# A two-layer decoder step: the first loads in another order, and the working area moved by one small tensor

## The chip, the cores and the metric

One core of a Trainium2 chip runs the whole step as one program. The metric is the device time in microseconds of one execution, the median of several; the profile comes from one further execution.

## What is computed

Two layers of a hybrid decoder, for one prompt of 256 tokens and 8 decode requests of one token each, so 264 rows of width 1024, all in float32. Cut to what matters here:

```python
q, k, v, z, xbc, dt = jnp.split(x @ w_in, IN_SPLITS, axis=-1)
q = _rope(q.reshape(b, L, 2 * ATT_HEADS, ATT_QK_DIM), pos)
k = _rope(k.reshape(b, L, 2 * ATT_HEADS, ATT_QK_DIM), pos)
...
dt = jax.nn.softplus(dt.astype(jnp.float32) + dt_bias.astype(jnp.float32))
...
mk, mv = jnp.split(mem @ w_ckv, 2, axis=-1)
...
logits = (x @ w_router).astype(jnp.float32)      # layer 1 only
top_v, top_i = lax.top_k(logits, TOP_K)
```

A layer is the mixer (differential attention beside a state space model, both from one input projection), cross-attention over 256 memory rows, and a feed-forward stage: dense in layer 0, the two best of eight experts in layer 1. Each of the three ends in a layer norm.

## The kernel before

Five engines run five hand-written instruction lists that meet at semaphores. TensorE (PE) multiplies, VectorE (DVE), ScalarE (ACT) and GpSimd (POOL) work on the results, and SyncE (SP) issues the loads. All weights pass through `ring`, six slots of 16 KB in each partition; `ring_chunks` lists the chunks in order and, for each, after which group of products its slot is free again. Results of TensorE go through eight PSUM banks; `psum_groups` lists the groups in order, with the engine (`"V"` or `"A"`) that empties each, and group n waits until group n - 8 has been emptied. So the order of both lists is the order of the work.

The start is this. SP issues `const` (identity, masks, cosines: 564 KB), the layer norm and convolution vectors into `vraw` (six small DMAs), x (slot 0), the memory rows (slot 1), the page table `ptab`, the q columns of `w_in` (slot 2), then nine small loads that all count on `small_landed` (the per-head parameters `raw8` and `col8`, the lambda parameters `lraw`, the time step weights `wdt` of both layers and the router's weights `wr`), then the columns k, xbc0, xbc1, the pages of cached keys, v and z. TensorE waits for `const` and the vectors, transposes the vectors (`vec`), x (`xin`, five groups by `blocks8`) and the memory rows (`mem`, four groups). Then the mixer begins: `token_major` multiplies the columns q and k by the decode rows and by two tiles of 128 prompt rows (`DECODE_FIRST` is that order: 2, 0, 1). After the decode rows of q come the time step products `dt`, 48 of 8 columns and 16 more, which wait for `small_landed`. After k come the cumulative sums (`acs`), and then eight blocks of xbc with the scores over the cached keys between them.

DVE copies `xin` to `xT` and spreads the decode rows over `xs` (`decode_columns`, line 2333). ACT copies `mem` to `memT`. Both then wait for `small_landed` for the parameters' set-up. GpSimd sets buffers to zero, waits for `const`, loads the convolution state (line 889), rotates q and k once they are there (lines 902 to 907), and stores k.

Most of the later time is products of layer 1's experts: their weights are cut into a high and a low part by ACT (line 1772) and DVE (line 2155), and TensorE (line 1216 is the line of all products, line 1220 of all transposes) multiplies three pairs of parts. The tiles of that stage lie in `arena`, the working area, which the stages of the kernel use in turn. `x_high`, `x_low` and `first_high` of layer 0's feed-forward stage lie in `arena` also; `high` lies in `R`, `SQ` and `memT`. The tensors stand one behind another in the order of their declarations.

Of the kernel before, what the change touches and what calls it, by code (L numbers as in the profile page):

```python
# [27 lines left out]
I32 = mybir.dt.int32  # L28
ALU = mybir.AluOpType
# [358 lines left out]
def build(nc, a, outs, lots=SLOTS, always=False):  # L388
# [3 lines left out]
    with ExitStack() as ctx:  # L392
# [67 lines left out]
        vraw = carve(2 * P, 0).rearrange("p (a n) -> p a n", a=2)  # L460
        lraw = carve(L * 4 * DQ).rearrange("p (l a d) -> p l a d", l=L, a=4)
# [144 lines left out]
        psum_full, emptied_by_act, emptied_by_dve = sem("psum_full"), sem("emptied_by_act"), sem("emptied_by_dve")  # L606
        const_landed, vecs_landed, small_landed, ptab_landed = (
# [77 lines left out]
        def _(sp):  # L685
            sp.dma_start(const[:], a["consts"]).then_inc(const_landed, 16)
            for j, (src, r0) in enumerate((
                    (a["ln_g"].rearrange("l i (k n) -> (l i k) n", n=P), 0),
                    (a["ln_b"].rearrange("l i (k n) -> (l i k) n", n=P), 48),
                    (a["ssm_norm_w"].rearrange("l (k n) -> (l k) n", n=P), 96),  # L690
                    (a["attn_norm_w"], 104),
                    (a["conv_b"].rearrange("l (k n) -> (l k) n", n=P), 106))):
                sp.dma_start(vraw[r0:r0 + src.shape[0], 0, :], src).then_inc(vecs_landed, 16)
            sp.dma_start(vraw[0:64, 1, :], a["conv_w"].rearrange("l i (k n) -> (l i k) n", n=P)
                         ).then_inc(vecs_landed, 16)
# [26 lines left out]
            for l in range(L):  # L722
                w_in = a["w_in"][l]
                columns((l, "q"), w_in, 0)
                if l == 0:
                    for i, n in enumerate(("dt_bias", "a_log", "d_skip")):
                        sp.dma_start(raw8[:, i], a[n].partition_broadcast(P)).then_inc(small_landed, 16)  # L727
                    with nc.allow_non_contiguous_dma(reason="sixteen words"):
                        for i, n in enumerate(("dt_bias", "a_log")):
                            sp.dma_start(col8[:, i, :], a[n].rearrange("l h -> h l")).then_inc(small_landed, 16)  # L730
                    sp.dma_start(lraw, a["lambda_params"].partition_broadcast(P)).then_inc(small_landed, 16)
# [4 lines left out]
                for key, c0 in (("k", 512), ("xbc0", 2048), ("xbc1", 2560)):  # L736
                    columns((l, key), w_in, c0)
# [2052 lines left out]
```

## Time and profile before

| | us |
|---|---|
| median of three runs | 1812.07 (1811.1 to 1814.3) |
| the profiled execution | 1809.09 |
| its span, from first to last instruction | 1807.2 |

The profiled execution was faster than the three timed ones. Its granted TensorE clock was 0.993 on average. TensorE was busy for 97% of the span, DVE 68%, ACT 47%, GpSimd 6%. The chain of work that ended last is followed back from the last instruction to what released each step; a timeline lists an engine's work in order, and ends a line with what the engine had waited for; a table by stretches gives each engine's busy time, the granted clock as a share of 2.4 GHz, and what the DMA engines did.

### The profile page before, as it was taken

How to read it: one execution, taken by the hardware profiler on the slowest of the kernel's cores; microseconds unless marked ns; L12 is line 12 of the kernel's file. 1: busy time of each engine (PE TensorE's matmuls, PEld its weight loads, DVE VectorE, ACT ScalarE, POOL GpSimd, SP SyncE). 2: the span in 40 equal slices, each digit the busy share in tenths (PEclk: the TensorE clock that was granted, in tenths of full speed). 3: DMA queues.
4: the chain of work that ended last, by engine and by line, in shares of the span. 5: the costliest groups of instructions: out<-in, count | busy, mean ns of one | idle time of the engine just before them, and what ended most of it. 6: DMA issues, size and time to landing. Idle time of an engine off the chain costs nothing.

```text
span 1807.2 us, 24014 instructions
## 1 busy us (share of the span) xinstructions
PE 1760.1 (97%) x8760; PEld 1360.8 (75%) x8760; DVE 1225.6 (68%) x1739; ACT 852.8 (47%) x978; POOL 112.2 (6%) x120
## 2 busy tenths in 40 slices
PE   7999999999999999999999999999999999999998
PEld 4646587789999565568677878878888878878786
DVE  2687636255544288543626989898988989898984
ACT  1122211154442122302205777777777777777774
POOL 0530000000000332000001000000000000000000
PEclk9999999999999999999998999999999999999999
DMA  9556544845526455563682989999999999999980
GB/s 323 183 199 212 215 185 169 285 158 181 175 83 228 137 185 171 187 262 123 233 279 96 358 279 356 345 348 352 349 376 324 377 324 363 337 350 352 348 335 26
DMA packets 300436, 459.34 MB, mean 254 GB/s; under 512 B 10879, under 2 KB 213817, under 8 KB 300343
## 3 DMA queue, kind: packets, MB, share of 16 engines
q1 hardware_dynamic: 294630, 442.63, 71.6%
q0 software_dynamic: 3424, 11.50, 1.9%
q10 hardware_dynamic: 2304, 4.20, 0.6%
q8 instruction: 47, 0.77, 0.2%
q14 instruction: 31, 0.25, 0.0%
HBM read 444.97 MB, written 13.46 MB: 254 GB/s over the span
## 4 chain that ended last, share of the span: by engine, by line
PE 86%; DVE 7%; ACT 3%; issue 1%; DMA 1%; SPq 1%; POOL 0%; ACTq 0%; DVEq 0%; POOLq 0%
PE bank L1216 83%; PE bank L1220 3%; DVE arena L2682 1%; DVE ring_low L2155 1%; ACT high L1772 1%; DMA out<-mem_rows 1%; DVE R L2296 1%; ACT L1772 0%; ACT arena L1840 0%; POOL arena L964 0%; ACT ye_high L1808 0%; ACT SQ L1861 0%; DVE st L2654 0%; DVE st L2575 0%; SPq L727 0%
## 5 line engine op out<-in xcount | busy, mean ns | idle before, releaser
L2155 DVE TENSOR_TENSOR ring_low<-ring,high 128x2048 fp32r<-128x2048 f32 x264 | 603.0, 2292 | 87.0 <-ACT high L1772 84.0
L1772 ACT ACTIVATE high<-ring 128x2048 fp32r<-128x2048 f32 x264 | 505.3, 1917 | 110.7 <-PE bank L1216 101.5
L1216 PE MATMUL bank<-high,xg_high 128*128 128x512 f32 x704 | 285.0, 405 | 6.2 <-DVE ring_low L2155 5.8
L1216 PE MATMUL bank<-ring_low,xg_high 128*128 128x512 f32 x704 | 278.5, 396 | 0.0
L1216 PE MATMUL bank<-high,xg_low 128*128 128x512 f32 x704 | 278.2, 395 | 0.0
L1216 PEld LDWEIGHTS bank<-high,xg_high 128*128 128x128 f32 x704 | 132.4, 188 | 36.3 <-DVE ring_low L2155 7.3
L1216 PEld LDWEIGHTS bank<-ring_low,xg_high 128*128 128x128 f32 x704 | 132.2, 188 | 31.7
L1216 PEld LDWEIGHTS bank<-high,xg_low 128*128 128x128 f32 x704 | 132.5, 188 | 28.4
L1840 ACT ACTIVATE arena<-bank 128x512 f32<-128x512 f32 (+3 forms) x95 | 46.4, 525 | 218.4 <-PE bank L1216 142.8
L1216 PE MATMUL bank<-high,he_high 128*128 128x512 f32 x352 | 141.8, 403 | 0.0
L1216 PE MATMUL bank<-ring_low,he_high 128*128 128x512 f32 x352 | 139.2, 396 | 0.0
L1216 PE MATMUL bank<-high,he_low 128*128 128x512 f32 x352 | 139.1, 395 | 0.0
L2273 DVE TENSOR_TENSOR ring_low<-ring,high 128x2048 fp32r<-128x2048 f32 (+1 forms) x32 | 71.1, 2225 | 92.6 <-ACT high L1849 92.6
L1216 PE MATMUL bank<-xT,ring 128*128 128x264 f32 x512 | 120.3, 391 | 0.8 <-ACT xT L1876 0.8
L1216 PE MATMUL bank<-SQ,ring 128*128 128x264 f32 x512 | 116.6, 391 | 0.9 <-issue 0.7
L1216 PE MATMUL bank<-ring,xT 128*128 128x512 f32 x256 | 116.5, 613 | 0.0
L1216 PE MATMUL bank<-ring,memT 128*128 128x512 f32 x256 | 113.3, 595 | 0.0
L1216 PEld LDWEIGHTS bank<-SQ,ring 128*128 128x128 f32 x512 | 98.1, 192 | 18.7 <-DVE SQ L2643 0.9
L1216 PEld LDWEIGHTS bank<-xT,ring 128*128 128x128 f32 x512 | 95.2, 190 | 21.9 <-issue 4.4
L1216 PE MATMUL bank<-x_high,ring_low 128*128 128x264 f32 x352 | 99.9, 284 | 0.0
L1849 ACT ACTIVATE high<-ring 128x2048 fp32r<-128x2048 f32 (+1 forms) x32 | 59.6, 1864 | 82.9 <-PE bank L1216 82.0
L1216 PEld LDWEIGHTS bank<-ring,xT 128*128 128x128 f32 x256 | 49.3, 196 | 62.6 <-issue 62.5
(327 smaller groups left out, 2613.2 us busy)
## 6 DMA issues: line engine op xcount, KB each, us to landing
ring<-in_w_exp_gu SPq DMA_DIRECT2D x176, 1024.0 KB, 11.3
ring<-in_w_exp_down SPq DMA_DIRECT2D x40, 2048.0 KB, 14.2
ring<-in_w_in SPq DMA_DIRECT2D x12, 2048.0 KB, 9.7
ring<-in_w_ffn_gu SPq DMA_DIRECT2D x22, 1024.0 KB, 8.5
ring<-in_w_ckv SPq DMA_DIRECT2D x8, 2048.0 KB, 8.6
ring<-in_cache_mem_k SPq DMA_DIRECT2D x16, 1024.0 KB, 8.1
ring<-in_cache_mem_v SPq DMA_DIRECT2D x16, 1024.0 KB, 6.6
ring<-in_cache_attn_k SPq DMA_DIRECT2D x32, 256.0 KB, 3.5
```

The source lines that it names most:

```text
L1216: return M.matmul(out, lhsT, rhs, start=start, stop=stop)
L1220: return M.transpose(out, in_, ident[0:n, 0:n])
L1772: S.activation(high_bufs[h % HIGH_BUFS][:], ring[:, s, j * HALF:(j + 1) * HALF], ACT.Copy).then_inc(split_high, 1)
L1840: emptied_after(name, S.activation(dst, src(bk), func))
L1849: S.activation(high, ring[:, s, part], ACT.Copy).then_inc(ffn_high, 1)
L2155: V.tensor_tensor(ring_low[:, s, part], ring[:, s, part], high_bufs[h % HIGH_BUFS][:], ALU.subtract).then_inc(split_low, 1)
L2273: V.tensor_tensor(ring_low[:, s, part], ring[:, s, part], high, ALU.subtract).then_inc(ffn_low, 1)
L2296: V.scalar_tensor_tensor(R[:, k, :], R[:, k, :], col_g(l, i, k), stat[:], ALU.mult, ALU.mult).then_inc(scaled.sem, 1)
L2682: ins = V.scalar_tensor_tensor(ctmp[:, (2 * t + j) * MD:(2 * t + j + 1) * MD], Kb[:, t, h * MD:(h + 1) * MD], 1.0, bk[:, j * MD:(j + 1) * ...
```

## The change

SP loads the identity alone, then x, then q. The rest of `const` and the vectors follow q, then k, and the memory rows and the page table follow k. The memory rows are the fourth chunk of the ring instead of the second. GpSimd issues seven of the nine small loads, at its start (layer 0's time step weights first); the other two, layer 1's time step weights and the router's, it issues after layer 0's rotated keys, and they count on `thin_landed`, for which layer 1 waits. TensorE transposes x first, and the vectors and the memory rows between k and the cumulative sums; their copies by DVE and ACT move along, and so do the copy of `pick` and the scaling of the attention norm. `dt` stands behind the first prompt tile of q, in both layers. ACT copies two of the five groups of x. `vraw` lies at the end of the working area, and `slot_token`, four bytes in each partition, is declared behind `arena` instead of ahead of it. The diff, cut:

```diff
 def psum_groups():
-    g = [(("vec",), "V")]
-    g += [(("xin", n), "V") for n in range(5)] + [(("mem", n), "A") for n in range(4)]
+    g = [(("xin", n), "A" if n in (1, 3) else "V") for n in range(5)]
...
-                if c == "q" and t == DECODE_FIRST[0]:
+                if c == "q" and t == DECODE_FIRST[1]:
                     add("V", "dt")
+                if l == 0 and c == "k" and t == DECODE_FIRST[-1]:
+                    g += [(("vec",), "V")] + [(("mem", n), "A") for n in range(4)]
...
 def ring_chunks():
-    c = [(("x",), 2, "pe", ("xin", 4)), (("mem",), 1, "pe", ("mem", 3))]
+    c = [(("x",), 2, "pe", ("xin", 4))]
     for l in range(L):
-        c += [((l, n), 1, "pe", (l, "tok", n, DECODE_FIRST[-1])) for n in ("q", "k")]
+        c += [((l, "q"), 1, "pe", (l, "tok", "q", DECODE_FIRST[-1]))]
+        c += [((l, "k"), 1, "pe", (l, "tok", "k", DECODE_FIRST[-1]))]
+        if l == 0:
+            c += [(("mem",), 1, "pe", ("mem", 3))]
...
-        slot_token = sb("slot_token", [P, 1], I32)
         x_rows = nc.dram_tensor("x_rows", [T, D], F32).ap()
         arena = sb("arena", [P, ARENA])
+        slot_token = sb("slot_token", [P, 1], I32)
...
-        vraw = carve(2 * P, 0).rearrange("p (a n) -> p a n", a=2)
-        lraw = carve(L * 4 * DQ).rearrange("p (l a d) -> p l a d", l=L, a=4)
+        vraw = carve(2 * P, ARENA - 2 * P).rearrange("p (a n) -> p a n", a=2)
+        lraw = carve(L * 4 * DQ, 0).rearrange("p (l a d) -> p l a d", l=L, a=4)
...
         @block.sync
         def _(sp):
-            sp.dma_start(const[:], a["consts"]).then_inc(const_landed, 16)
-            for j, (src, r0) in enumerate((
...
+            sp.dma_start(const[:, C_ID:C_ID + P], a["consts"][:, C_ID:C_ID + P]).then_inc(ident_landed, 16)
             s = rg.claim(sp, ("x",))
...
-            s = rg.claim(sp, ("mem",))
-            sp.dma_start(ring[:, s, 0:2048].rearrange("p (t n) -> p t n", t=2),
-                         a["mem_prompt"].rearrange("o (t p) n -> p (o t) n", p=P)).then_inc(landed[s], 16)
-            sp.dma_start(ptab[:], a["page_table"].rearrange("b g -> (b g)").unsqueeze(0)).then_inc(ptab_landed, 16)
+            def first_vectors():
+                sp.dma_start(const[:, C_ID + P:NCONST], a["consts"][:, C_ID + P:NCONST]).then_inc(const_landed, 16)
...
+            def memory_rows():
+                s = rg.claim(sp, ("mem",))
...
                 columns((l, "q"), w_in, 0)
                 if l == 0:
-                    for i, n in enumerate(("dt_bias", "a_log", "d_skip")):
-                        sp.dma_start(raw8[:, i], a[n].partition_broadcast(P)).then_inc(small_landed, 16)
...
-                    for n in range(L):
-                        sp.dma_start(wdt[:, n], a["w_in"][n, :, 3072:3080].rearrange("(k p) n -> p k n", p=P)
-                                     ).then_inc(small_landed, 16)
-                    sp.dma_start(wr[:], a["w_router"][0].rearrange("(k p) n -> p k n", p=P)).then_inc(small_landed, 16)
-                for key, c0 in (("k", 512), ("xbc0", 2048), ("xbc1", 2560)):
+                    first_vectors()
+                columns((l, "k"), w_in, 512)
+                if l == 0:
+                    memory_rows()
+                for key, c0 in (("xbc0", 2048), ("xbc1", 2560)):
                     columns((l, key), w_in, c0)
...
             G.memset(xpad[:, :, 0:3], 0.0).then_inc(buffers_set, 1)
+            def time_step_weights(n, landed_by):
+                pool.dma_start(wdt[:, n], a["w_in"][n, :, 3072:3080].rearrange("(k p) n -> p k n", p=P)
+                               ).then_inc(landed_by, 16)
+            time_step_weights(0, small_landed)
+            for i, n in enumerate(("dt_bias", "a_log", "d_skip")):
+                pool.dma_start(raw8[:, i], a[n].partition_broadcast(P)).then_inc(small_landed, 16)
...
+            pool.dma_start(lraw, a["lambda_params"].partition_broadcast(P)).then_inc(small_landed, 16)
             pool.wait_ge(const_landed, 16)
...
                 store(o_ks[l, :, 0].rearrange("b h d -> b (h d)"), qkr[0:8, 2, 512:1024])
+                if l == 0:
+                    time_step_weights(1, thin_landed)
+                    pool.dma_start(wr[:], a["w_router"][0].rearrange("(k p) n -> p k n", p=P)).then_inc(thin_landed, 16)
...
-            pe.wait_ge(const_landed, 16)
-            pe.wait_ge(vecs_landed, 16 * 6)
...
+            pe.wait_ge(ident_landed, 16)
             blocks8(("xin",), slot(("x",))[:, 0:3072].rearrange("p (t n) -> p t n", t=3))
...
                         token_major(c, t, first)
-                        if first:
-                            pe.wait_ge(small_landed, 16 * 9)
+                        if c == "q" and t == DECODE_FIRST[1]:
+                            pe.wait_ge(*((thin_landed, 16 * 2) if l else (small_landed, 16 * 7)))
                             bk = turns.open(pe, (l, "dt"))
...
+                    if l == 0 and c == "k":
+                        vector_columns()
+                        memory_columns()
                 bk = turns.open(pe, (l, "acs"))
+                pe.wait_ge(const_landed, 16)
...
-            for n in range(4):
-                copy_out(("mem", n), memT[:, 4 * (n % 2):4 * (n % 2) + 4, (n // 2) * P:(n // 2 + 1) * P],
+            for n in (1, 3):
+                copy_out(("xin", n), xT[:, 4:8, (n // 2) * P:(n // 2 + 1) * P],
                          lambda bk: bk[:].rearrange("p (k n) -> p k n", k=4))
-            act.wait_ge(small_landed, 16 * 9)
+            act.wait_ge(small_landed, 16 * 7)
...
+                if l == 0:
+                    bk = take(dve, ("vec",))
+                    step.inc(V.tensor_copy(vecT[:, 0, 0:122], bk[:, 0:122]))
+                    emptied_after(("vec",), V.tensor_copy(vecT[:, 1, 0:64], bk[:, 128:192]))
...
```

## Rows read from the trace of the kernel before

**Rows 1.** The page, part 4: shares of the chain that ended last, by engine.

```profile
PE 86%; DVE 7%; ACT 3%; issue 1%; DMA 1%; SPq 1%; POOL 0%; ACTq 0%; DVEq 0%; POOLq 0%
```

**Rows 2.** The chain that ended last, in order of time: start us, us, what.

```profile
17.43 4.01 DMA wr<-in_w_router
21.48 38.04 PE bank L1216 x152
...
64.16 44.71 PE bank L1216 x184
...
252.99 1.75 PE bank L1220 x16
```

**Rows 3.** Timeline of SP's queue: start us, us, line, operation, out<-in, count.

```profile
0.76 0.42 SPq L686 DMA_DIRECT2D const<-in_consts  x1
...
3.83 0.58 SPq L697 DMA_DIRECT2D ring<-in_x_prompt  x1
...
6.09 2.90 SPq L727 DMA_DIRECT2D raw<-in_dt_bias  x1
...
25.84 21.71 SPq L718 DMA_DIRECT2D ring<-in_cache_attn_k  x16
```

**Rows 4.** Timeline of PE, first 60 us, and one row of layer 1.

```profile
9.67 8.23 PE L1220 MATMUL bank<-const,ring 128*128 128x128 f32 x40 [3.17 <-DMA ring<-in_x_sample]
18.79 1.92 PE L1216 MATMUL bank<-ring,mem_rows 128*32 128x512 f32 x16 [0.89 <-issue]
21.48 4.43 PE L1216 MATMUL bank<-wdt,xT 128*128 128x8 f32 x48 [0.77 <-DMA wr<-in_w_router]
...
26.25 16.68 PE L1216 MATMUL bank<-ring,xT 128*128 128x512 f32 x32
42.86 1.92 PE L1216 MATMUL bank<-ring,mem_rows 128*32 128x512 f32 x16
44.72 14.00 PE L1216 MATMUL bank<-ring,xT 128*128 128x512 f32 x32
...
595.70 4.54 PE L1216 MATMUL bank<-ring,xT 128*128 128x512 f32 x7
```

**Rows 5.** Timeline of DVE: the decode rows' columns.

```profile
14.59 0.20 DVE L2333 COPY mem_rows<-xT 128x64 f32<-128x64 f32 x1
```

**Rows 6.** Stretches of the start: busy us of each engine, granted clock, DMA share, GB/s.

```profile
6.00:9.00 3.00, 0.50 (x2) 0.18 (x1) 0.58 (x3) 0.00 (x0) 0.29 (x1) 1.00 1.03 397
9.00:12.00 3.00, 2.33 (x11) 2.33 (x12) 1.01 (x2) 0.00 (x0) 0.00 (x0) 1.00 0.99 295
12.50:17.00 4.50, 4.50 (x25) 4.15 (x25) 1.81 (x4) 1.20 (x2) 0.00 (x0) 1.00 1.05 386
17.00:18.00 1.00, 0.90 (x5) 0.50 (x3) 0.00 (x0) 0.66 (x2) 0.00 (x0) 1.00 1.11 354
18.00:21.00 3.00, 1.92 (x16) 0.50 (x16) 0.00 (x0) 0.54 (x1) 0.00 (x0) 1.00 0.88 104
```

**Rows 7.** Stretches again, for the clock, in the same columns.

```profile
9.70:13.10 3.40, 3.40 (x16) 3.25 (x16) 1.95 (x3) 0.00 (x0) 0.00 (x0) 1.00 1.02 322
...
24.90:31.60 6.70, 6.70 (x42) 3.54 (x43) 3.41 (x10) 0.80 (x3) 0.00 (x0) 0.50 1.05 393
...
594.90:598.20 3.30, 3.30 (x35) 1.94 (x35) 1.00 (x6) 0.46 (x2) 0.00 (x0) 0.50 0.33 90
```

**Rows 8.** POOL's timeline, and of the same line its DMAs' time from issue to landing.

```profile
5.02 0.72 POOL L889 DMA_DIRECT2D SQ<-in_state_conv  x1 [2.94 <-DMA const<-in_consts]
...
DMA to landing us min/median/max: 6.0/6.6/7.2
```

**Rows 9.** Tile x_high: duration of its products in ns, min/median/max.

```profile
L1216 PE MATMUL bank<-x_high,high x320: 279/283/290, 392.4 to 508.6; 128*128 128x264 f32 x160
...
L1216 PE MATMUL bank<-x_high,first_high x32: 281/284/361, 380.6 to 392.1; 128*128 128x264 f32 x32
```

**Rows 10.** The page, part 5: one of the groups of the experts' products.

```profile
L1216 PE MATMUL bank<-high,xg_high 128*128 128x512 f32 x704 | 285.0, 405 | 6.2 <-DVE ring_low L2155 5.8
```

More of the change, by code:

```diff
@@ L883, in _ @@
             G.memset(xpad[:, :, 0:3], 0.0).then_inc(buffers_set, 1)
+            def time_step_weights(n, landed_by):
[4 more added lines that the diff above has]
+                pool.dma_start(raw8[:, i], a[n].partition_broadcast(P)).then_inc(small_landed, 16)
+            with nc.allow_non_contiguous_dma(reason="sixteen words"):
+                for i, n in enumerate(("dt_bias", "a_log")):
+                    pool.dma_start(col8[:, i, :], a[n].rearrange("l h -> h l")).then_inc(small_landed, 16)
+            pool.dma_start(lraw, a["lambda_params"].partition_broadcast(P)).then_inc(small_landed, 16)
             pool.wait_ge(const_landed, 16)
@@ L1321, in x_ready, with vector_columns, memory_columns @@
                 return ready
-            pe.wait_ge(const_landed, 16)
-            pe.wait_ge(vecs_landed, 16 * 6)
-            bk = turns.open(pe, ("vec",))
-            tr(bk[:, 0:122], vraw[0:122, 0, :], 122)
-            full(tr(bk[:, 128:192], vraw[0:64, 1, :], 64))
-            blocks8(("xin",), slot(("x",))[:, 0:3072].rearrange("p (t n) -> p t n", t=3))
-            mem_in = slot(("mem",))[:, 0:2048].rearrange("p (t n) -> p t n", t=2)
-            for n in range(4):
-                bk = turns.open(pe, ("mem", n))
-                for j in range(4):
-                    k = 4 * (n % 2) + j
-                    last = tr(bk[:, j * P:(j + 1) * P], mem_in[:, n // 2, k * P:(k + 1) * P], P)
-                full(last)
+            pe.wait_ge(ident_landed, 16)
+            blocks8(("xin",), slot(("x",))[:, 0:3072].rearrange("p (t n) -> p t n", t=3))
+            def vector_columns():
+                pe.wait_ge(vecs_landed, 16 * 6)
+                bk = turns.open(pe, ("vec",))
+                tr(bk[:, 0:122], vraw[0:122, 0, :], 122)
+                full(tr(bk[:, 128:192], vraw[0:64, 1, :], 64))
+            def memory_columns():
+                mem_in = slot(("mem",))[:, 0:2048].rearrange("p (t n) -> p t n", t=2)
+                for n in range(4):
+                    bk = turns.open(pe, ("mem", n))
+                    for j in range(4):
+                        k = 4 * (n % 2) + j
+                        last = tr(bk[:, j * P:(j + 1) * P], mem_in[:, n // 2, k * P:(k + 1) * P], P)
+                    full(last)
+            copied(pe, ("xin", 3))
             pe.wait_ge(buffers_set, 6)
@@ L1880, in _ @@
             S.preload_act_table_set(EXP_AND_LN)
-            for n in range(4):
-                copy_out(("mem", n), memT[:, 4 * (n % 2):4 * (n % 2) + 4, (n // 2) * P:(n // 2 + 1) * P],
+            for n in (1, 3):
+                copy_out(("xin", n), xT[:, 4:8, (n // 2) * P:(n // 2 + 1) * P],
                          lambda bk: bk[:].rearrange("p (k n) -> p k n", k=4))
-            act.wait_ge(small_landed, 16 * 9)
+            act.wait_ge(small_landed, 16 * 7)
             step.inc(S.activation(raw8[:, 1], raw8[:, 1], ACT.Exp))
@@ L1913, in _ @@
                             copy_out((l, "tok", name, t), qk_raw[:, t, 512 * c:512 * (c + 1)], lambda bk: bk[:])
+                    if l == 0 and c == 1:
+                        for n in range(4):
+                            copy_out(("mem", n), memT[:, 4 * (n % 2):4 * (n % 2) + 4, (n // 2) * P:(n // 2 + 1) * P],
+                                     lambda bk: bk[:].rearrange("p (k n) -> p k n", k=4))
                 decays_in.wait(act, l)
@@ L2318, in _ @@
             step.inc(V.memset(xs, 0.0))
-            bk = take(dve, ("vec",))
-            step.done(V.tensor_copy(pick[:], const[0:40, C_PICK:C_PICK + 8]))
-            step.inc(V.tensor_copy(vecT[:, 0, 0:122], bk[:, 0:122]))
-            emptied_after(("vec",), V.tensor_copy(vecT[:, 1, 0:64], bk[:, 128:192]))
-            for n in range(5):
+            for n in (0, 2, 4):
                 t, bk = n // 2, take(dve, ("xin", n))
@@ L2326, in _ @@
                 nk = 8 if t == 2 else 4
-                k0 = 0 if t == 2 else 4 * (n % 2)
                 emptied_after(("xin", n), V.tensor_copy(
-                    xT[:, k0:k0 + nk, t0:t0 + rows], bk[:, 0:nk * rows].rearrange("p (k n) -> p k n", k=nk)))
+                    xT[:, 0:nk, t0:t0 + rows], bk[:, 0:nk * rows].rearrange("p (k n) -> p k n", k=nk)))
             def decode_columns(l):
@@ L2391, in _ @@
                 other_quarters(1, "k", qk_raw[0:8, 2, 512:1024])
+                if l == 0:
+                    bk = take(dve, ("vec",))
+                    step.inc(V.tensor_copy(vecT[:, 0, 0:122], bk[:, 0:122]))
+                    emptied_after(("vec",), V.tensor_copy(vecT[:, 1, 0:64], bk[:, 128:192]))
+                    dve.wait_ge(const_landed, 16)
+                    step.done(V.tensor_copy(pick[:], const[0:40, C_PICK:C_PICK + 8]))
+                    for n in range(L):
+                        step.inc(V.tensor_scalar(col_attn(n), col_attn(n), 1.0 - LAM_INIT[n], None, ALU.mult))
                 bk = take(dve, (l, "acs"))
```

31 lines of the change are left out of this document (16 added, 15 removed).

## The prediction

> **What bounds the kernel now.** I read the chain of work that ended last first: 86% of the span is TensorE [Rows 1]. Nearly all of it is products behind one another, so a change of loads can only pay where TensorE waits for a load. Followed from its start, the chain is SP's queue and then the router's weight load `wr`, issued at 17.43 and in use at 21.48; from there it is TensorE without a break for 38.04 us, and again for 44.71 us from 64.16 [Rows 2]. So the only stretch that this change can shorten ends at 21.48, and what it adds to TensorE's own work between 21.48 and 58.7 costs its full length. After that SP issues a load when TensorE frees a slot, so the rest of the kernel should move as one block with the end of k.
>
> Second, the timelines. SP issues `const` at 0.76, seven DMAs on x at 3.83, and the first load after q at 6.09 [Rows 3]. TensorE transposes x and the memory rows from 9.67 to 17.9, begins q at 18.79, stops 0.77 us at the time step weights (`dt`), and goes on at 21.48 [Rows 4]. The decode columns that q needs were ready at 14.79 [Rows 5], so the wait up to 18.79 is for q's bytes. The stretches by DMA rate say the same: 295 to 397 GB/s until 18, then 104 GB/s [Rows 6]. The DMA engines are full until q is in, and x's consumer waits for x. The start is bound by bytes in front of q and by SP's order, not by TensorE.
>
> Third, the clock. The 16 transposes between 9.7 and 13.1 took 3.40 us, 0.21 us each [Rows 7], against 0.109 us at 252.99 (16 in 1.75 us) [Rows 2]. They ran at 1.2 GHz, although the column says 1.00 there (I take it that no change had been recorded yet). The first q products took 1.92 us, as those at 42.86 did [Rows 4], so 2.4 GHz had been reached by then. After the narrow `dt` products the granted clock is 0.50 from 24.9 to 31.6 [Rows 7]: two prompt tiles of q take 16.68 us where k's two take 14.00 [Rows 4], 2.68 us lost. In layer 1 the same happens from 594.9 to 598.2 [Rows 7], while full products run from 595.70 [Rows 4], which is about 1.3 us lost.
>
> **x earlier.** Only the identity (64 KB, one issue like const's 0.42 us) stays before x, so x is issued at about 0.76 + 0.42 + 0.05 = 1.23 instead of 3.83 [Rows 3]. All behind it moves by 2.6 us: x is used at 7.07 instead of 9.67, and the decode columns are ready at 12.2 instead of 14.8 [Rows 4, 5]. ScalarE's two copies of x take the place of DVE's and cost nothing: ScalarE has only its table load before.
>
> **q earlier.** The 1 MB of memory rows and `const` leave the way before q. The last q byte to the first product took 18.79 - 18.0 = 0.8 us [Rows 4, 6]; x's last byte then lies near 7.07 - 0.8 = 6.3. q is 2.1 MB, at 386 to 397 GB/s [Rows 6] 5.4 us, so it is usable at 6.3 + 5.4 + 0.8 = 12.5 if nothing else runs. But GpSimd now issues seven loads from 2.1 us on (it idles from there, 2.94 us before 5.02 [Rows 8]), and they share the engines with x and q: 0.3 MB, of which 1024 pieces of 32 bytes. At q's rate that is 0.7 us. From above: with the three loads of such small pieces in it, 18 to 21 moved at 104 GB/s, so one of the three cost about 1 us; and from 9 to 12, while GpSimd's own two DMAs ran, the rate was 295 instead of 390, which over q's 5.4 us is 1.8 us; with lambda's 0.7, 3.5 in all. I take 1.6, nearer to the low end since the measured dip lasted 3 us. q starts at **14.1** (12.5 to 16.0) instead of 18.79: **4.7 us won** (2.8 to 6.3).
>
> **dt without the wait.** The router's weights and layer 1's time step weights are no longer waited for: 0.77 us won [Rows 4]. `dt` now stands behind a prompt tile of q, so it is wanted at about 14.1 + 1.9 + 7.0 + 2 = 25. GpSimd's issue of a small load took 0.72 us and its landing 6.0 to 7.2 us [Rows 8]: seven issues end near 2.1 + 7 x 0.72 = 7.1, and land near 14.3. Cover is 10 us. ScalarE and DVE wait for them too, with only q's decode quarter behind that wait; its bank is not wanted back before eight more groups. The work of `dt`, 21.48 to 26.25, stays as long in its new place, in both layers.
>
> **Transposes onto the path.** The 16 of the memory rows and the two of the vectors lay under the wait for q; now they stand between k and the cumulative sums, with nothing to hide them: 16 x 0.109 = 1.75 [Rows 2] and about 0.3 for the two others, **2.05 lost**. Their copies (four of ScalarE, two and three small ones of DVE) run beside them and beside the sums, and are free unless ScalarE's last copy delays its one exponential there, some tenths.
>
> **The clock.** Transposes of x alone last 4.4 us instead of 8.2, and 2 us without work follow, so I expect q to begin at 1.2 GHz. Price: the stretches after `dt`, 2.7 and 1.3 us, mean **2.0 lost** (0 to 2.7). After `dt` the clock should fall as before; its mean price is 2.0, 0.7 less than what this profile paid: **0.7 won** (0 to 1.4).
>
> The Trainium skill (TensorE: Matmul & The Clock Gate, Part 4) says that transposes don't count as busy for the clock. Here they did: nothing but transposes ran from 9.67 to 17.9, and the products behind them were at full speed [Rows 4]. By the page, q would have begun slow in the kernel before also, and this term would be 0.
>
> **Slots.** x, q, k and memory rows now lie in slots 0 to 3. The second half of the cached keys waits for q's slot, free near 38; eight of the 16 pages take half of 21.71 us [Rows 3], so they are issued by 49, before k ends. v waits for k's slot, and is read only after the stretch that began at 64.16 [Rows 2]. GpSimd's two later loads stand behind the rotation, before its wait for the state; SP no longer issues them. All nothing.
>
> **The working area.** Each tensor starts at a multiple of 32 bytes; by the sizes, `arena` starts 32 bytes past a multiple of 64 and would start on one. In the feed-forward stage weights that lie in `arena` (`first_high`) and weights on multiples of 64 (`high`) meet the same moving rows: 284 and 283 ns [Rows 9]. The moving rows of 1056 bytes lie by turns on and off such a multiple, and all of them take 279 to 293 ns. So 0 to 1 ns; over the experts' three groups of 704 and three of 352 products [Rows 10] at most 3.2 us won. No row shows a loss from either start. I take 0.
>
> **Sum.** 4.7 + 0.77 - 2.05 - 2.0 + 0.7 = **2.1 us won**. The profiled run took 1809.09 us (span 1807.2), so it would take 1807.0; the median of the runs shown is 3 us above it, and 1812.07 - 2.1 gives **1810.0**. Best ends together: 6.3 + 0.77 - 2.05 + 1.4 = 6.4 won, 1805.7. Worst ends: 2.8 + 0.77 - 2.05 - 2.7 = -1.2, 1813.3.
>
> **Rivals.** (a) *The start pays in full*: GpSimd's loads fall behind q, or the clock rises in x's transposes. 5 to 6.4 us, **about 1806.5**. For it: q at 12.5 needs only the bytes; against it the dip at 9 to 12 [Rows 6].
> (b) *GpSimd's queue takes the place of `wr`* (slower): seven loads through its queue, waited for together. Should each take its 6.6 us after the one before, the last lands at 2.1 + 46 = 48, 23 us after `dt` wants it: **1833**. It decides from 25 us on, and from 31 on the kernel is slower by more than can be told. Against it: 10 us of cover. The Trainium skill (DMA: Bandwidth & Descriptors, Issuing engine by pattern) speaks for it: simple loads belong on SP, whose path is generally faster than GpSimd's. In this trace GpSimd's load needs 7.2 us with x and q in flight, which agrees.
> (c) *q isn't earlier at all*, since it is the DMA engines that count and GpSimd's small pieces cost what the memory rows did: only the transposes move, 2.05 - 0.77 = 1.3 lost, **1813.4**.
> (d) *The working area's start matters* where no row here shows it: experts' products with their weights there. 3 us or more, **1807 or below**.
>
> **Chances.** Forecast 0.53, (a) 0.22, (b) 0.08, (c) 0.11, (d) 0.06. About 0.2%, 3.6 us, is what a measurement of this kernel can tell from no change. Faster: most of (a) and (d) and a little of the forecast, 0.30. Slower: (b) and a tail of (c), 0.11. Within: 0.59. The range, 1804 to 1815, reaches from (a) with some of (d) to past (c) and leaves out most of (b).
>
> **What would show it.** Right: x transposed from 7, q's first product near 14, `dt` without idle time before it, 16 transposes of about 1.8 us after k, k's end 2 us earlier than 58.7, and every later stage moved by as much. Wrong: idle time before `dt` with GpSimd's loads as releaser (b), q at 17 or later (c), expert products spaced otherwise than before (d), or a granted clock that stays at 0.50 beyond one prompt tile.

## The result, and the profile after

| | kernel before | changed kernel |
|---|---|---|
| median, us | 1811.92 (1811.1 to 1814.3) | 1796.83 (1795.31 to 1800.61) |
| profiled execution, us | 1809.09 | 1800.61 |
| its span, us | 1807.2 | 1798.7 |

The changed kernel is 15 us faster: ratio 0.9916, 95% interval 0.9900 to 0.9932. That is below the predicted range (1804 to 1815), and the time wasn't won where the prediction looked for it. The profiled execution was the slowest of the four of the changed kernel; what it has more than a profiled execution of a kernel with the same loads is named below.

First the start. This is TensorE's timeline after (start us, us, engine, line, operation, out<-in, count, and in brackets the idle time before it with its releaser); it answers to [rows 4].

```profile
7.22 4.41 PE L1240 MATMUL bank<-const,ring 128*128 128x128 f32 x24 [7.22 <-DMA ring<-in_x_sample]
16.75 3.64 PE L1236 MATMUL bank<-ring,mem_rows 128*32 128x512 f32 x16 [5.12 <-DMA ring<-in_w_in]
20.32 7.69 PE L1236 MATMUL bank<-ring,xT 128*128 128x512 f32 x16
27.86 4.12 PE L1236 MATMUL bank<-wdt,xT 128*128 128x8 f32 x48
...
56.45 0.47 PE L1240 MATMUL bank<-const,arena 122*128 122x122 f32 x2
...
58.66 0.51 PE L1236 MATMUL bank<-st,const 128*128 128x8 f32 x4
...
65.89 0.47 PE L1236 MATMUL bank<-pair_in,pick 40*128 40x512 f32 x1 [1.92 <-DVE pair_in L2352]
```

x is used at 7.22 instead of 9.67 and q begins at 16.75 instead of 18.79, after 5.12 us in which TensorE waits for q's bytes. Nothing is idle ahead of `dt`. The transposes that now stand behind k lead to the cumulative sums at 58.66; before, that row began at 58.55. All that the loads won in the first 17 us was gone by then.

Next, the tile `xg_high` (gathered token rows of the experts) in both kernels: the duration of its products in ns, min/median/max, and when the first and the last began. The first line is of the kernel before, the second of the changed kernel.

```profile
L1216 PE MATMUL bank<-high,xg_high x704: 392/396/503, 977.2 to 1745.1; 128*128 128x512 f32 x176
```

```profile
L1236 PE MATMUL bank<-high,xg_high x704: 386/389/497, 984.0 to 1737.4; 128*128 128x512 f32 x176
```

The experts begin 6.8 us later than before, and their last such product begins 7.7 us earlier: the stage between takes 753.4 instead of 767.9 us. The shortest, the median and the longest product are all 6 to 7 ns shorter. The page's groups say it with the mean of one in ns behind the busy time; first the changed kernel, then two groups of the kernel before ([rows 10] has a third, 405 ns).

```profile
L1236 PE MATMUL bank<-high,xg_high 128*128 128x512 f32 x704 | 281.9, 400 | 7.3 <-DVE ring_low L2192 6.9
L1236 PE MATMUL bank<-ring_low,xg_high 128*128 128x512 f32 x704 | 275.4, 391 | 0.0
L1236 PE MATMUL bank<-high,xg_low 128*128 128x512 f32 x704 | 274.5, 390 | 0.0
L1236 PE MATMUL bank<-high,he_low 128*128 128x512 f32 x352 | 137.3, 390 | 0.0
```

```profile
L1216 PE MATMUL bank<-high,xg_low 128*128 128x512 f32 x704 | 278.2, 395 | 0.0
L1216 PE MATMUL bank<-high,he_low 128*128 128x512 f32 x352 | 139.1, 395 | 0.0
```

Some 5 ns less for each of 3 x 704 + 3 x 352 = 3168 products is 15.8 us, the whole result. No other stage shows it in its means: the dense stage's products, which have 264 columns instead of 512, take 283 to 284 ns in the changed kernel also, as in [rows 9].

One rival lies in the trace: VectorE and ScalarE read and write the weights' buffers while TensorE reads them, and they could be what the products meet. Near the end of the experts there is a stretch in which both stand still, and the products differ there as they do elsewhere. First that stretch and its products in the kernel before, then in the changed one (stretch; busy us and instructions of PE, PEld (TensorE's loads of stationary rows), DVE, ACT, POOL; granted clock; DMA share; GB/s).

```profile
1775.41:1778.67 3.26, 3.26 (x15) 2.63 (x14) 0.00 (x0) 0.00 (x0) 0.00 (x0) 1.00 0.02 5
L1216 PE MATMUL bank<-high,he_low x5: 395/396/396, 1775.6 to 1778.4; 128*128 128x512 f32 x5
```

```profile
1767.02:1770.19 3.17, 3.17 (x15) 2.63 (x14) 0.00 (x0) 0.00 (x0) 0.00 (x0) 1.00 0.02 5
L1236 PE MATMUL bank<-high,he_low x5: 388/389/390, 1767.2 to 1770.0; 128*128 128x512 f32 x5
```

So the 6 ns don't need the other engines.

The 6.8 us by which the experts begin later come mostly from three places in this one execution. The wait for `pair_in` at 65.89 is 1.92 us instead of 0.3; the wait for the memory keys' rows, on the chain, is longer; and TensorE's granted clock was 0.51 in two stretches in which it was 1.00 before, the first of them after TensorE had stood idle for 2.10 us. Here are that wait and the products behind it in the chain of the changed kernel (start us, us, what; before, the wait took 6.04 us and the products 8.92), and the two stretches (columns as above).

```profile
205.37 7.91 DMA out<-mem_rows
215.45 10.57 PE bank L1236 x32
```

```profile
216.00:219.50 3.50, 3.50 (x16) 2.98 (x15) 1.74 (x4) 0.00 (x0) 0.00 (x0) 0.51 0.66 263
318.40:321.90 3.50, 3.50 (x13) 2.93 (x12) 3.40 (x19) 0.25 (x1) 0.00 (x0) 0.51 1.02 412
```

The first of the two stretches cost 1.65 us (the 32 products behind the wait took 10.57 instead of 8.92), and over the second the lag behind the kernel before grew by 1.2 us on the chain, from 5.2 to 6.4. With 1.6 for `pair_in` and 1.9 for the wait that is 6.3 of the 6.8. The experiments show an execution with the same loads that has none of the three.

### The profile page after: what moved, and what is told of

It reads as the page before. It is cut to its first block, busy times and chain, and to the rows that moved or that the text cites. A ratio compares the mean times of both kernels' runs of the same rounds, so it can differ in the third digit from the quotient of the medians.

```text
span 1798.7 us, 24015 instructions
## 1 busy us (share of the span) xinstructions
PE 1746.6 (97%) x8760; PEld 1361.9 (76%) x8760; DVE 1226.2 (68%) x1737; ACT 853.4 (47%) x980; POOL 117.8 (7%) x129
## 4 chain that ended last, share of the span: by engine, by line
PE 86%; DVE 7%; ACT 3%; DMA 2%; issue 1%; POOL 0%; ACTq 0%; SPq 0%; DVEq 0%; POOLq 0%
PE bank L1236 83%; PE bank L1240 3%; DVE arena L2721 1%; DVE ring_low L2192 1%; DMA out<-mem_rows 1%; DMA ring<-in_w_in 1%; ACT high L1805 1%; DVE R L2333 1%; ACT L1805 0%; ACT arena L1873 0%; POOL arena L984 0%; ACT ye_high L1841 0%; ACT SQ L1894 0%; DVE st L2614 0%; DVE st L2693 0%
## 5 line engine op out<-in xcount | busy, mean ns | idle before, releaser
L1236 PE MATMUL bank<-high,xg_low 128*128 128x512 f32 x704 | 274.5, 390 | 0.0
## 6 DMA issues: line engine op xcount, KB each, us to landing
ring<-in_w_in SPq DMA_DIRECT2D x12, 2048.0 KB, 14.3
```

The lines of the kernel that those rows point to most:

```text
L1236: return M.matmul(out, lhsT, rhs, start=start, stop=stop)
```

## The experiments

The kernel before was measured again beside each group of experiments; its median there was 1809.4 to 1812.6 us. The seven kernels that move tiles inside the working area, the moving rows or all tensors ran once each, so what they show is read from their products' rows, not from their times.

**The two halves of the change.** The theories: the loads (L) or the working area's start (W). The first kernel is the kernel before with one line moved:

```diff
-        slot_token = sb("slot_token", [P, 1], I32)
         x_rows = nc.dram_tensor("x_rows", [T, D], F32).ap()
         arena = sb("arena", [P, ARENA])
+        slot_token = sb("slot_token", [P, 1], I32)
```

> The kernel before with one line moved: slot_token is declared behind arena, so that arena starts on a multiple of 64 bytes; loads as before. Theory W (the experts' products read their weights faster when these start on such a multiple): the spacing of the experts' products falls from about 232 to 228 ns, one pass of 24 products from 5.59 to 5.47 us, the expert stage is about 16 us shorter, and all of the gain is here or more: 0.989 to 0.992 of before. Theory L (the order of the loads makes the gain, and the product spacing follows from it): no change, 1.000. Theory S (both, in halves): 0.995.

Measured: 1797.55 us, ratio 0.9917 (0.9900 to 0.9933), where the changed kernel had 0.9916. One of its product groups:

```profile
L1216 PE MATMUL bank<-high,xg_high 128*128 128x512 f32 x704 | 281.9, 400 | 7.4 <-DVE ring_low L2155 7.0 <-DVE xg_low L2147 0.4
```

The second is the changed kernel with that line put back, so only the loads are new:

> The changed kernel with slot_token back ahead of arena: new loads, old place of the working area. Theory W: spacing back at 232 ns, and the start gives nothing or costs: TensorE's first stage as late as in the changed kernel's trace (first cross stage 1.7 us later than before), 1.000 to 1.004 of before. Theory L: 0.992. My prediction's own sum, without the working area: 0.9988 (2.1 us won).

Measured: 1813.39 us, ratio 1.0010 (0.9998 to 1.0022). Product groups and TensorE's timeline of the start:

```profile
L1236 PE MATMUL bank<-high,xg_low 128*128 128x512 f32 x704 | 278.2, 395 | 0.0
L1236 PE MATMUL bank<-high,he_low 128*128 128x512 f32 x352 | 139.1, 395 | 0.0
```

```profile
15.95 3.64 PE L1236 MATMUL bank<-ring,mem_rows 128*32 128x512 f32 x16 [4.38 <-DMA ring<-in_w_in]
19.52 8.29 PE L1236 MATMUL bank<-ring,xT 128*128 128x512 f32 x16
...
32.09 8.83 PE L1236 MATMUL bank<-ring,xT 128*128 128x512 f32 x16
...
58.75 0.51 PE L1236 MATMUL bank<-st,const 128*128 128x8 f32 x4
...
63.99 0.49 PE L1236 MATMUL bank<-pair_in,pick 40*128 40x512 f32 x1
```

The whole gain comes from `slot_token`, four bytes that no longer stand ahead of the working area; all the moved loads together are worth nothing that can be measured. At the cumulative sums and at the first cached-score product this kernel stands where the kernel before did, within 0.2 us (58.75 against 58.55, 63.99 against 64.16 [rows 2]), without a wait for `pair_in`: the loads alone don't bring that wait with them; it differs between profiled executions with the same loads.

**Which start, and on which grid.** Next, tiles inside the working area were moved on, with the changed kernel as the base. `xg` stands for `xg_high` and `xg_low`, the stationary rows of the experts' first products; `he` for `he_high` and `he_low`, those of the second; the moving rows are `high` (in R, SQ and `memT`) and `ring_low`. First xg by 32 bytes (8 words), and all behind it by 64:

```diff
+        carve(8)
         xg_high = parts_in("xg_high", "arena", used[0], [KT, P])
...
         carve(2 * KT * P)
+        carve(8)
```

> The changed kernel with xg_high and xg_low alone put 32 bytes further on, so 32 bytes past a multiple of 64; he_high, he_low and all else stay on multiples of 64. If the start of the weights decides, the 2112 products on xg go back to 231 to 235 ns (mean duration 395 to 405 ns in the groups, as before) and the 1056 on he stay at 227 (390 to 397). If the start of another tile decides (moved rows, sums, buffers), neither moves.

Measured: 1813.11 us; xg is slow as expected (395 ns for `high,xg_low`), but he too:

```profile
L1238 PE MATMUL bank<-high,he_low 128*128 128x512 f32 x352 | 138.8, 394 | 0.0
```

So the grid isn't 64 bytes, or one misplaced tile slows the other's products. Beside it, the moving side was misplaced instead: the two `high` buffers in R and SQ by 32 bytes, the one in `memT` left alone.

```diff
-        high_bufs = [parts_in(f"high{n}", host, 0, [HALF]) for n, host in enumerate(("R", "SQ", "memT"))]
+        high_bufs = [parts_in(n, host, at, [HALF]) for n, host, at in (
+            ("off_r", "R", 8), ("off_sq", "SQ", 8), ("high2", "memT", 0))]
```

> The changed kernel with two of the three buffers of the high parts (in R and SQ) put 32 bytes further on; the third, in memT, stays on a multiple of 64. In the experts these are the moving rows, in the dense feed-forward stage the weights. If the moving operand's start matters as the weights' does, experts' products on off_r and off_sq take some 5 ns more than those on high2; if only the weights' start matters, all take the same, 390 to 400 ns mean duration, and the dense stage stays at 157.7 us or gets some 1 us longer.

Measured: 1809.77 us. Of the products with `xg_low`, those that read a misplaced buffer take 396 ns and those of the third buffer 391; `he_low` shows the same, 395 against 389:

```profile
L1237 PE MATMUL bank<-off_r,xg_low 128*128 128x512 f32 x256 | 101.3, 396 | 0.0
L1237 PE MATMUL bank<-high,xg_low 128*128 128x512 f32 x224 | 87.6, 391 | 0.0
```

So the moving side counts as well. But the products with `xg_high` don't separate by buffer: the median is 394 ns for all three, and 393 for `ring_low,xg_high`, none of whose operands was moved; in the changed kernel both rows have 389. Here are the third buffer's and `ring_low`'s (min/median/max):

```profile
L1237 PE MATMUL bank<-high,xg_high x224: 388/394/505, 990.2 to 1743.5; 128*128 128x512 f32 x112
L1237 PE MATMUL bank<-ring_low,xg_high x704: 387/393/401, 984.6 to 1746.7; 128*128 128x512 f32 x176
```

So part of the loss falls on products whose own operands are in place. The theories below don't say why.

Then xg by 64 (`carve(16)` ahead of it and 16 behind) and by 32 (8 and 24), both with all behind it moved by 128 bytes, so that he stands on a multiple of 128:

> The changed kernel with the experts' token rows (xg_high, xg_low) moved on by 64 bytes and everything behind them by 128 bytes in all: xg starts 64 bytes past a multiple of 128, the hidden rows (he_high, he_low) on a multiple of 128. If 128 bytes is the grid that counts: the three groups of 704 products with xg go back to 405, 396 and 395 ns, the three of 352 with he stay at 397, 390 and 390, and the kernel takes 1797 + 704 x 16 ns = 1808 us. If it was 64 bytes, and the slow he of the kernel with xg moved by 32 bytes came from something else: all six groups stay at 390 to 400, 1797 us. If a start more than 64 bytes further on is what hurts he: both slow, 1813.

> The same with xg moved on by 32 bytes and everything behind it by 128 bytes in all. xg starts 32 bytes past a multiple of 128, he on one. If each operand's own start counts, on a grid of 128 bytes: xg at 405, 395, 395 and he at 397, 390, 390; 1808 us. If one misplaced operand slows all of the stage: both slow, 1813.

Measured: 1810.91 and 1811.08 us, everything slow in both, and a grid of 128 bytes for each operand's own start falls. In the first of the two the rows of he, which stand on a multiple of 128, are slow too:

```profile
L1238 PE MATMUL bank<-high,he_low 128*128 128x512 f32 x352 | 138.9, 395 | 0.0
```

```diff
+        ahead = sb("ahead", [P, 8])
         ring = sb("ring", [P, RING, SLOT])
```

> The changed kernel with 32 bytes of padding ahead of the ring, so that every tensor behind it (ring, R, SQ, memT, the working area) starts 32 bytes later and their places relative to each other stay as they are. If the distance between the start of the stationary rows (xg, he) and that of the moving rows (ring, R, SQ, memT) is what counts, a multiple of 256 bytes being fast: 400, 391, 390 and 397, 391, 390 as before the padding, spacing 227 ns, about 1797 us. If each operand's own start counts, against a fixed grid: 405, 396, 395 and 403, 396, 395, 1813 us.

The other moves xg by 128 bytes and he by 256 (`carve(32)` ahead of xg and behind it):

> The changed kernel with xg moved on by 128 bytes and everything behind it by 256 bytes in all. If the distance counts, and 256 bytes is its grid: xg slow (405, 396, 395), he fast (397, 391, 390), 1808 us. If each operand's own start counts on a grid of 128 bytes, or the distance does on one of 128: all fast, 1797 us. If one misplaced operand slows the whole stage: all slow, 1813 us.

Measured: 1794.65 and 1802.91 us. First the kernel with the padding, then the other:

```profile
L1237 PE MATMUL bank<-high,xg_low 128*128 128x512 f32 x704 | 274.4, 390 | 0.0
L1237 PE MATMUL bank<-high,he_low 128*128 128x512 f32 x352 | 137.3, 390 | 0.0
```

```profile
L1238 PE MATMUL bank<-high,xg_low 128*128 128x512 f32 x704 | 277.8, 395 | 0.0
L1238 PE MATMUL bank<-high,he_low 128*128 128x512 f32 x352 | 137.0, 389 | 0.0
```

With every tensor 32 bytes further on, all stays fast: it is not each operand's own start that matters. With xg at a distance of 128 and he at 256, xg alone is slow: neither does one tile slow the other. Of the theories here only the distance is left, and a multiple of 256 bytes is fast. All kernels of these pairs in one table (distance to the moving rows, modulo 256; mean ns of `high,xg_low` and `high,he_low`):

| kernel | xg | he | xg ns | he ns |
|---|---|---|---|---|
| before; loads alone | 32 | 32 | 395 | 395 |
| changed; move alone; all moved by 32 | 0 | 0 | 390 | 390 |
| xg by 32, he by 64 | 32 | 64 | 395 | 394 |
| xg by 64, he by 128 | 64 | 128 | 395 | 395 |
| xg by 32, he by 128 | 32 | 128 | 395 | 395 |
| xg by 128, he by 256 | 128 | 0 | 395 | 389 |
| moving rows in R and SQ by 32, products on these | 224 | 224 | 396 | 395 |
| the same kernel, products on `memT` | 0 | 0 | 391 | 389 |

Last, which of the two reads meets which. While a product's moving rows run, TensorE loads the next product's stationary rows (of the changed kernel, start us, us):

```profile
1767.25 0.39 PE L1236 MATMUL bank<-high,he_low 128*128 128x512 f32 x1
1767.25 0.19 PEld L1236 LDWEIGHTS bank<-ring_low,he_high 128*128 128x128 f32 x1
1767.47 0.39 PE L1236 MATMUL bank<-ring_low,he_high 128*128 128x512 f32 x1
```

The order of xg's products is high,xg_high; high,xg_low; ring_low,xg_high. So `xg_low` alone was moved by 32 bytes (and he by 256):

```diff
-        xg_low = parts_in("xg_low", "arena", used[0] + KT * P, [KT, P])
-        carve(2 * KT * P)
+        xg_low = parts_in("xg_low", "arena", used[0] + KT * P + 8, [KT, P])
+        carve(2 * KT * P + 64)
```

> The changed kernel with xg_low alone moved on by 32 bytes and everything behind it by 256 bytes; xg_high and the hidden rows keep a distance from the moving rows that is a multiple of 256 bytes. The products of a row block come in the order high,xg_high; high,xg_low; ring_low,xg_high, and while one runs, TensorE loads the stationary rows of the next. If the weight load of the misplaced rows collides with the product that runs meanwhile: high,xg_high goes to 405 ns, the other two stay at 391 and 390. If a product's own two operands count: high,xg_low goes to 395, the other two stay. If a collision shifts the next ones too: all three are 2 to 5 ns longer. Either way 704 to 2112 products by some 5 ns, 3.5 to 10 us: 1800 to 1807 us. The he groups stay at 397, 391 and 390.

Measured: 1804.15 us.

```profile
L1236 PE MATMUL bank<-high,xg_high 128*128 128x512 f32 x704 | 286.5, 407 | 6.2 <-DVE ring_low L2192 5.9 <-DVE xg_low L2184 0.4
L1236 PE MATMUL bank<-ring_low,xg_high 128*128 128x512 f32 x704 | 277.9, 395 | 0.0
L1236 PE MATMUL bank<-high,xg_low 128*128 128x512 f32 x704 | 274.9, 390 | 0.0
```

The product with the misplaced rows keeps its 390 ns. The one during which they are loaded, high,xg_high, goes from 400 to 407. That is what a collision of the load of the next stationary rows with the moving rows of the running product would do, but it isn't shown: ring_low,xg_high, beside which only well placed rows are loaded, pays 4 ns as well, and in the kernel with the misplaced moving rows well placed products paid too. A product's record also lasts 0.39 us where the next product starts after 0.22, so that one product's loss can stand in its neighbour's record. That the distance counts is shown; how the loss comes about is open.

**What holds q back.** In the changed kernel the DMA rate was 338 and 344 GB/s from 3 to 7 us and fell to 209 from 7 to 11 us, while the loads that GpSimd had issued from 2.02 us on were moving. In these 4 us GpSimd's queue (q0) moved 0.09 MB and SP's (q1) 0.75 MB, and q0's packets took 42.5% of the DMA engines' time (queue, kind: packets, MB, share of 16 engines):

```profile
q1 hardware_dynamic: 364, 0.75, 59.5%
q0 software_dynamic: 176, 0.09, 42.5%
```

So the seven small loads were taken from GpSimd and issued by SP behind q:

```diff
-            time_step_weights(0, small_landed)
...
                 columns((l, "q"), w_in, 0)
                 if l == 0:
+                    small_loads()
                     first_vectors()
```

> The changed kernel, with the seven small loads of the time step weights and per-head constants issued by SP right behind q instead of by GpSimd from 2 us on; layer 1's and the router's stay with GpSimd. If GpSimd's small loads took the rate from q: 9 to 13 us moves at 380 GB/s or more, q's first product begins at 12.5 to 13.5 instead of 16.75, dt has no wait, k ends at 54.5 to 55.5 instead of 58.66. Then the kernel takes 3 to 4 us less, 1793, if the rest moves as one block; 1796 to 1797 if the later stages give it back, as they did with 6 us of the changed kernel between 64 and 984 us. If the rate fell for another reason (q's own many rows): q at 16.5 or later, 1797.

Measured: 1794.22 us (1792.59 to 1798.26), ratio 0.9906 (0.9888 to 0.9925). The rate of a start stretch, and TensorE's timeline:

```profile
9.00:12.00 3.00, 2.77 (x17) 2.34 (x15) 0.88 (x2) 1.19 (x2) 0.00 (x0) 1.00 1.10 334
```

```profile
12.95 3.64 PE L1241 MATMUL bank<-ring,mem_rows 128*32 128x512 f32 x16 [1.17 <-DMA ring<-in_w_in]
...
55.76 0.51 PE L1241 MATMUL bank<-st,const 128*128 128x8 f32 x4
```

q begins at 12.95, 3.8 us earlier than in the changed kernel, and the cumulative sums at 55.76, 2.9 us earlier. In all ten profiles here of kernels with GpSimd's loads at the start q begins between 15.81 and 17.00, in the two with SP's at 12.93 and 12.95. GpSimd's seven loads were what held q back. The edit also delays the rest of `const`, the vectors and k, which SP now issues from 10.74 us on instead of 2.59. These don't explain it: in the changed kernel the first packet of the rest of `const` moved at 13.11 us, when q was late already. Of the 380 GB/s that I expected, 334 were reached. The whole time can't be told from the changed kernel's: the intervals of the two ratios overlap for the most part.

**pair_in.** VectorE splits the decode rows of q ahead of the vectors' bank and the sums, when GpSimd has just rotated them (`pick` is converted before that):

```diff
                 other_quarters(1, "k", qk_raw[0:8, 2, 512:1024])
+                rope_ready.wait(dve, l, 0)
+                split_rows(qkr[0:8, 2, 0:512], pair_in).then_inc(pair_ready.sem, 1)
```

> The changed kernel with only the second of the two edits: VectorE splits the decode rows of q (pair_in) before the vectors' bank and the cumulative sums, in both layers. The wait of 1.92 us for pair_in ahead of the first cached-score product goes, so that product begins 3.8 us after the first of the 16 products before it: 1.5 to 2 us less than the changed kernel's 1796.8, near 1795, if the rest moves as one block; 1796.8 if a later wait takes it up.

Measured: 1795.80 us (1795.16 to 1799.55), ratio 0.9906 (0.9879 to 0.9933). The wait is gone, but against the changed kernel's 1796.83 that is no difference that can be told, and some profiled executions without this edit don't have the wait either, as that of the loads alone shows.

Both edits together:

> As the one before, and VectorE splits the decode rows of q (pair_in) before it takes the vectors' bank and the cumulative sums, in both layers, so that its two instructions don't run beside GpSimd's rotation and behind six others; pick is converted earlier for it. In layer 0 TensorE waited 1.92 us for pair_in at 65.89: that wait goes, the first cached-score product stands right behind the 16 products before it, 1.9 us earlier than without this step. If the rest moves as one block 1.5 to 2 us less than without it, near 1791; if the next wait (the scores' consumer, VectorE) takes it up, no difference.

Measured: 1790.72 us (1789.28 to 1791.53), ratio 0.9888 (0.9869 to 0.9906): every run is below every one of the changed kernel's and of the kernel with the first edit alone. It is the fastest kernel here. Against the first edit alone, measured beside it, that is a difference; the ratio's interval still touches the changed kernel's (0.9900 to 0.9932). TensorE's first cached-score product, the row at 65.89 of the changed kernel, stands at 60.57 without a wait:

```profile
60.57 0.49 PE L1241 MATMUL bank<-pair_in,pick 40*128 40x512 f32 x1
```

Of the 3.5 us between it and the kernel with the first edit alone, 1.3 us lie before this product (61.90 there). The rest isn't settled: in the profile of the other kernel the granted clock fell in three stretches (63, 213 and 316 us) where this one kept 1.00.

## Why the prediction was wrong

**The working area: the step that failed.** The forecast put it at 0 to 1 ns for each product, at most 3.2 us, and took 0. It is 5 ns, and 15 us. The bound came from [rows 9], the products with `x_high` as the moving rows, and their means couldn't show it: the rows are 1056 bytes long, 4 x 256 + 32, so the distance to any stationary row steps through eight values whatever the starts are, and over the whole stage they took 283 to 284 ns with either start. (The prediction's "279 to 293 ns" leaves out one of 361 in [rows 9].) Row by row they do differ. Worked out from the starts in the traces, the products with `x_low` as the moving rows and `high` as the stationary ones follow one another after 117.8 to 124.2 ns, by which of the eight rows it is. The quickest is the fourth row in the kernel before and with the loads alone, and the eighth in the changed kernel, with the move alone and with everything moved by 32 bytes; the mean over the eight rows is 121.4 or 121.5 in all five. Two things should have made the bound wider: the row had 264 columns where the products to be priced have 512, and the question asked of it was each tile's start (off or on a multiple of 64) when two operands are read at a time. "No row shows a loss from either start" was true, and no evidence. Rival (d) named the right products and the right sign, their spacing, with "3 us or more, 1807 or below" and a chance of 0.06; its size was never worked out, so the range stopped at 1804. All other steps together moved the time by nothing that can be told (1.0010).

**x earlier: right.** Predicted 7.07, measured 7.22.

**q earlier: mis-sized.** 4.7 us won was forecast, q at 14.1 (12.5 to 16.0). It began at 16.75 in the changed kernel and 15.95 with the loads alone, 2.0 to 2.8 us won. The term that failed is GpSimd's loads at 1.6 us: without them q begins at 12.95, so they cost 3.0 to 3.8 in these two, around the upper of the two bounds (3.5). The choice of the low end, since the dip of before lasted 3 us, was the mistake: with seven loads instead of two the rate was 209 GB/s for 4 us, not 295 for 3. The bytes alone were right: 12.5 predicted, 12.95 measured. The Trainium skill (DMA: Bandwidth & Descriptors, Issuing engine by pattern) puts simple loads on SP's path and calls it generally faster than GpSimd's; the 3.8 us between 16.75 and 12.95 agree.

**dt: right.** No wait, and rival (b) is out. GpSimd issued its loads from 2.02 to 6.5 and ScalarE's and VectorE's wait for them ended at 13.95, where 14.3 was predicted.

**Transposes behind k: right.** 2.05 predicted, 2.21 measured (56.45 to 58.66).

**The clock: right in the changed kernel's profile, 0.9 short with the loads alone.** The decode rows of q took 3.64 instead of 1.92 [rows 4], 1.7 lost; the two prompt tiles 7.69 + 8.53 = 16.2 instead of 16.68, 0.5 won. -1.3 was the forecast (-2.0 and +0.7), and -1.2 to -1.3 came. With the loads alone the same products took 2.2 us more than before, inside the forecast's bounds. In the changed kernel's stretches the granted clock is 1.00 right behind x's transposes and 0.50 after TensorE has stood idle:

```profile
11.30:14.60 3.30, 0.33 (x5) 0.24 (x4) 1.04 (x5) 0.51 (x3) 0.00 (x0) 1.00 1.03 370
14.67:21.50 6.83, 4.75 (x18) 1.35 (x19) 2.81 (x25) 0.79 (x2) 1.07 (x2) 0.50 1.06 374
```

In this trace the clock rose while the transposes ran: the last eight, small ones, start 107 ns apart until 11.24 us and 62 ns apart from there, and nothing but transposes ran ahead. In the profile of the loads alone the same small transposes stay 107 ns apart to their end, and the clock rose only during q. The Trainium skill (TensorE: Matmul & The Clock Gate, Part 4) says that transposes don't count as busy. The rise at 11.24 disagrees with the page, as the kernel before did; the profile of the loads alone doesn't.

**The sum of the start.** With the loads alone: 2.8 + 0.8 - 2.2 for the transposes - 2.2 for its clock (3.64, 8.29 and 8.83 against 1.92 and 16.68) + 0.3 (`dt` itself a little shorter) = -0.5; measured at the cumulative sums, -0.2. Of the 2.3 us between that and the forecast of +2.1, 1.9 are q's. That rival (c)'s 1813.4 is what the loads alone measured (1813.39) is luck: (c) had q no earlier than before, and q was 2.8 us earlier; the transposes and the clock took it back.

## What to carry to other kernels

Where TensorE streams many 512-column products, look at the distance between stationary and moving operand in the address, not at either start: here a tensor of four bytes, which moved one of the two by 32, cost 0.8%, and a padding ahead of every tensor alike cost nothing. A bound for an unknown cost is worth as much as its row's likeness to the thing priced: a row with another shape, in whose mean the quantity cancels out, excludes nothing. Small loads on GpSimd's queue aren't free for the large one that runs meanwhile: seven of them, issued in 4.5 us, put q back by 3.0 to 3.8 us, and when SP issued them behind q, TensorE waited for none of them.

## What the runs showed of the hardware

- Experts' products (fp32r, 128 x 128 stationary, 512 moving columns) with `xg_low` and `he_low` take 389 to 391 ns on average when the stationary rows lie a multiple of 256 bytes from the moving rows, and 394 to 396 at distances of 32, 64, 128 and 224 bytes past one. The loss is as large at 128 as at 32. Other distances weren't tried. It is there with VectorE and ScalarE idle too (396 against 389).
- With `xg_low` alone misplaced, the product during its load went from 400 to 407 ns, its own stayed at 390, and ring_low,xg_high went from 391 to 395. With two of three buffers of moving rows misplaced, products on the third went from a median of 389 to 394 as well. How the loss comes about isn't shown.
- The 264-column products of the dense stage took 283 to 284 ns on average throughout, while the start of the working area decides which of their eight rows is quickest; whether rows of a length that is a multiple of 256 bytes would make them shorter wasn't tried.
- The DMA rate was 209 GB/s from 7 to 11 us with GpSimd's seven loads in flight, whose packets took 42.5% of the DMA engines' time for 0.09 of 0.84 MB; with these loads on SP it was 334 at 9 to 12.
- The granted clock was 0.51 in stretches of 3.5 us at 216 and at 318 in one execution, the first after TensorE had stood idle for 2.10 us; in that of the kernel with only the loads it stayed at 1.00 there, and the dense stage began at 381.1 instead of 387.0, with the two shorter waits in that difference.
